# An expert layer's gate and up products in whole 512-column chunks, with SiLU, product and transposes at 512 columns, and the working area moved to a multiple of 64 bytes

## The chip, the cores and the metric

One Trainium2 chip, one of its cores. The metric is the device time of one execution of the whole program in microseconds (us), lower is better.

## The reference

One step of a two-layer language model on 256 prompt tokens and 8 decode tokens, 264 in all, model width 1024, all in fp32. Each layer has a mixer (differential attention beside a state-space model), a cross-attention to a memory of 256 rows, and a channel part, each followed by a residual and a layer norm. The channel part of layer 0 is a dense SwiGLU of width 2816. That of layer 1 is a mixture of 8 experts with the two best experts of each token, and it is this part that the change touches:

```
def _swiglu(x, w_gu, w_down):
    g, u = jnp.split(x @ w_gu, 2, axis=-1)
    return (jax.nn.silu(g) * u) @ w_down

def _moe(x, w_router, w_exp_gu, w_exp_down):
    ...
    for e in range(N_EXPERTS):
        out = out + _swiglu(x, w_exp_gu[e], w_exp_down[e]) * gate[..., e:e + 1].astype(x.dtype)
```

`w_exp_gu` is 8 x 1024 x 5632 (the first 2816 columns are gate, the others up), `w_exp_down` is 8 x 2816 x 1024: 34.6 MB of weights for each expert.

## The kernel before

The engines run programs written out by hand and meet on semaphores. The first 960 us or so are the two mixers, the cross-attentions and the dense SwiGLU; the eight experts follow, one after the other, each in the same loop body (`expert` on every engine).

**Weights in chunks.** SyncE (SP) streams an expert's weights into a ring of six slots of 2 MB: 11 gate/up chunks (positions p = 0 to 10) and 6 down chunks (p = 11 to 16, the last one half as large). Gate/up chunk i holds 256 gate columns and the 256 up columns that belong to them, for all 1024 rows, fetched by two DMAs (`load`, L800 to L805), so that each contiguous run in memory is 256 words, 1 KB. A slot is loaded again when PE has used its chunk up (`expert_chunk_used`).

**Two parts of each weight.** To get fp32 products from the faster fp32r format, each chunk is split in halves of 2048 words per partition. ScalarE (ACT) rounds a half into one of three buffers (`high_part`, L1772), VectorE (DVE) subtracts that from the original in place (`low_part`, L2155), and TensorE (PE) takes three matmuls for each 128 rows: high x high, low activations x high weights, high activations x low weights (`product`). The three `high` buffers tie the engines together: ACT may fill the buffer of half h only when PE has used half h-3 up.

**One expert on PE.** `gate_up(f)` multiplies the expert's up to 128 gathered tokens (the stationary operands `xg_high`, `xg_low`) with chunk f (the moving operand, 512 columns): 24 matmuls into one of two PSUM banks in turn, of which columns 0 to 255 are gate and 256 to 511 up. ACT takes SiLU of the gate half into `sg` (`silu`, L1783), DVE multiplies it with the up half into `hh` (`multiply`, L2170), PE turns the result with two 128-column transposes into a T bank (`transpose_h`, L1220, after the next chunk's matmuls), ACT and DVE take the high and the low part of that (`take_h`, L1787; `low_of_h`, L2178) for the down product. `sg`, `hh` and the T banks have two buffers each. Then `down(0..5)` makes the output rows from the down chunks. In the first four chunks PE also scatters the previous expert's rows to their tokens (`scatter_before`, with moving operand `SelT`), and DVE adds them (`add_scattered`, L2160). At the end of an expert, ACT and DVE scale and split the down result (`ye_high` L1808, `ye_low` L2206).

**The next expert's tokens.** DVE makes a selection matrix (`next_slots`, L2139) at p = 5, PE multiplies it with the token numbers beside the transposes of f = 6, DVE writes `slot_token` (L2176), and GpSimd (POOL) fetches the rows with an indirect DMA (L973). PE transposes them before `down(4)`.

**Order on ACT and DVE.** For each position p both run `high_part(p)` or `low_part(p)` first, then the small work: `silu(p-1)` or `multiply(p-1)`, then `take_h(p-2)` or `low_of_h(p-2)`.

**Memory.** `sb()` puts the tensors one after the other. `arena` is the working area that holds, among others, `xg_high`, `xg_low`, `sg`, `hh`, `he_high`, `he_low`, `ye_high` and `SelT` in this part, and `x_high`, `x_low`, `h_high`, `h_low` in the dense SwiGLU. It begins right behind the 4-byte `slot_token`, which takes 32 bytes of each partition; so it begins 32 bytes behind a multiple of 64. `ring`, `R`, `SQ` and `memT` (the `high` buffers) begin at multiples of 64.

Of the kernel before, what the change touches and what calls it, by code (L numbers as in the profile page):

```python
# [27 lines left out]
I32 = mybir.dt.int32  # L28
ALU = mybir.AluOpType
# [3 lines left out]
P = 128  # L33
# [26 lines left out]
SLOT = 4096  # L60
EPOS = NGU + NDN + 1
# [326 lines left out]
def build(nc, a, outs, lots=SLOTS, always=False):  # L388
# [3 lines left out]
    with ExitStack() as ctx:  # L392
# [51 lines left out]
        slot_token = sb("slot_token", [P, 1], I32)  # L444
        x_rows = nc.dram_tensor("x_rows", [T, D], F32).ap()
        arena = sb("arena", [P, ARENA])
        banks = [ctx.enter_context(nc.psum_tensor(f"bank{i}", [P, 512], F32)) for i in range(8)]
# [79 lines left out]
        sg = carve(2 * GU).rearrange("p (s n) -> p s n", s=2)  # L527
        hh = carve(2 * GU).rearrange("p (s n) -> p s n", s=2)
# [156 lines left out]
        def _(sp):  # L685
# [362 lines left out]
        TOKEN_STEP = 6  # L1048
        SUM_BANKS = GU_BANKS + T_BANKS

        def expert_products(pe, mm, tr, warm):
# [39 lines left out]
            def expert(e, c):  # L1091
# [28 lines left out]
                def scatter_matrix():  # L1120

                    pe.wait_ge(T_done, i * NGU + NGU - 1)
                    pe.wait_ge(T_low, i * NGU + NGU - 1)
                    for t in range(3):
                        tr(T_BANKS[1][0:lots, t * P:(t + 1) * P], Sel[:, t, 0:lots], P)
                    for t in range(3):
                        last = mm(T_BANKS[1][0:lots, 3 * P:3 * P + 1], GSel[:, t, 0:lots], one_col[:], t == 0, t == 2)
                    last.then_inc(scatter_full, 1)

                def transpose_h(f):  # L1130
                    pe.wait_ge(h_ready, i * NGU + (f + 1))
                    if f >= 2:
                        pe.wait_ge(T_done, i * NGU + (f - 1))
                        pe.wait_ge(T_low, i * NGU + (f - 1))
                    for s in range(2):
                        last = tr(T_BANKS[f % 2][:, s * lots:(s + 1) * lots],
                                  hh[0:lots, f % 2, s * P:(s + 1) * P], lots)
                    if f == TOKEN_STEP:
                        pe.wait_ge(next_sel_ready, i + 1)
                        for t in range(3):  # L1140
                            last = mm(T_BANKS[f % 2][0:lots, 3 * P:3 * P + 1], next_sel[:, t, 0:lots],
                                      const[:, C_TOK + t:C_TOK + t + 1], t == 0, t == 2)
                    last.then_inc(T_full, 1)

                def down(d):
                    p = NGU + d
                    f_last = min(4 * d + 3, FT - 1) // 2
                    pe.wait_ge(T_done, i * NGU + (f_last + 1))
                    pe.wait_ge(T_low, i * NGU + (f_last + 1))
# [13 lines left out]
                for f in range(NGU):  # L1163
# [588 lines left out]
        def expert_activations(act):  # L1752
# [22 lines left out]
            def expert(e, c):  # L1775
                i = expert_no(e, c)

                def silu(f):
                    act.wait_ge(gu_full, i * NGU + (f + 1))
                    if f >= 2:  # L1780
# [4 lines left out]
                def take_h(f):  # L1785
                    act.wait_ge(T_full, i * NGU + (f + 1))
                    S.activation(he_high[:, 2 * f:2 * f + 2, 0:lots],  # L1787
                                 T_BANKS[f % 2][:, 0:2 * lots].rearrange("p (s n) -> p s n", s=2),
                                 ACT.Copy).then_inc(T_done, 1)

                for p in range(1, NGU + NDN):
                    high_part(e, c, p)
                    if 1 <= p <= NGU:
                        silu(p - 1)
                    if 2 <= p <= NGU + 1:
                        take_h(p - 2)
                    if p == NGU + 3:
                        act.wait_ge(scatter_full, i + 1)
                        S.activation(slot_gate[0:lots], T_BANKS[1][0:lots, 3 * P:3 * P + 1], ACT.Copy).then_inc(gate_ready, 1)
                        S.activation(SelT[0:lots, :], T_BANKS[1][0:lots, 0:T], ACT.Copy).then_inc(scatter_ready, 1)  # L1800
# [323 lines left out]
        def expert_elementwise(dve):  # L2124
# [37 lines left out]
            def expert(e, c):  # L2162
                i = expert_no(e, c)

                def multiply(f):
                    dve.wait_ge(sg_ready, i * NGU + (f + 1))
                    if f >= 2:

                        dve.wait_ge(T_full, i * NGU + (f - 1))
                    V.tensor_tensor(hh[0:lots, f % 2, :], sg[0:lots, f % 2, :], GU_BANKS[f % 2][0:lots, GU:2 * GU],  # L2170
                                    ALU.mult).then_inc(h_ready, 1)

                def low_of_h(f):
                    dve.wait_ge(T_done, i * NGU + (f + 1))
                    if f == TOKEN_STEP:
                        V.tensor_copy(slot_token[0:lots], T_BANKS[f % 2][0:lots, 3 * P:3 * P + 1]  # L2176
                                      ).then_inc(token_ready, 1)
                    V.tensor_tensor(he_low[:, 2 * f:2 * f + 2, 0:lots],  # L2178
                                    T_BANKS[f % 2][:, 0:2 * lots].rearrange("p (s n) -> p s n", s=2),
                                    he_high[:, 2 * f:2 * f + 2, 0:lots], ALU.subtract).then_inc(T_low, 1)  # L2180

                for p in range(1, NGU + NDN):
                    low_part(e, c, p)
                    if 1 <= p <= NGU:
                        multiply(p - 1)
# [5 lines left out]
                    if 2 <= p <= NGU + 1:  # L2191
                        low_of_h(p - 2)
                    if p == TOKEN_STEP - 1:
# [596 lines left out]
```

## Time and profile before

| | us |
|---|---|
| three runs, median | 1812.07 |
| three runs, lowest and highest | 1811.1 and 1814.3 |
| the profiled execution, whole time | 1809.09 |
| the profiled execution, span from first to last instruction | 1807.2 |

The profile is of one execution. Its span is 1807.2 us, and 1.9 us of its time lie outside it. "Busy" is the time in which an engine had an instruction running; matmuls are pipelined, each is shown some 0.4 us long while the next one starts after 0.23 us, so for PE the distance from start to start is the cost. "Idle before" and "waited for" name what ended an engine's wait. The expert part runs from about 977 to 1784 us.

### The profile page before, as it was taken

What the parts mean: (1) busy time and instruction counts of PE and PEld (TensorE: products, weight loads), DVE (VectorE), ACT (ScalarE), POOL (GpSimd) and SP (SyncE); (2) the same over time, 40 slices, a digit from 0 to 9 for tenths busy, and PEclk for the clock granted to TensorE, in tenths of its full rate; (3) what the DMA queues carried; (4) which work ended last, traced back from release to release, by engine and by line L of the source; (5) the groups of instructions that cost most, each with busy time, mean ns of one, the idle gap of its engine ahead of it and who ended that gap; (6) DMA issues with size and microseconds to landing.
All of it is one profiled execution on the core that took longest, in us unless ns stands there. A gap on an engine that the chain in (4) does not pass through costs nothing.

```text
span 1807.2 us, 24014 instructions
## 1 busy us (share of the span) xinstructions
PE 1760.1 (97%) x8760; PEld 1360.8 (75%) x8760; DVE 1225.6 (68%) x1739; ACT 852.8 (47%) x978; POOL 112.2 (6%) x120
## 2 busy tenths in 40 slices
PE   7999999999999999999999999999999999999998
PEld 4646587789999565568677878878888878878786
DVE  2687636255544288543626989898988989898984
ACT  1122211154442122302205777777777777777774
POOL 0530000000000332000001000000000000000000
PEclk9999999999999999999998999999999999999999
DMA  9556544845526455563682989999999999999980
GB/s 323 183 199 212 215 185 169 285 158 181 175 83 228 137 185 171 187 262 123 233 279 96 358 279 356 345 348 352 349 376 324 377 324 363 337 350 352 348 335 26
DMA packets 300436, 459.34 MB, mean 254 GB/s; under 512 B 10879, under 2 KB 213817, under 8 KB 300343
## 3 DMA queue, kind: packets, MB, share of 16 engines
q1 hardware_dynamic: 294630, 442.63, 71.6%
q0 software_dynamic: 3424, 11.50, 1.9%
q10 hardware_dynamic: 2304, 4.20, 0.6%
q8 instruction: 47, 0.77, 0.2%
q14 instruction: 31, 0.25, 0.0%
HBM read 444.97 MB, written 13.46 MB: 254 GB/s over the span
## 4 chain that ended last, share of the span: by engine, by line
PE 86%; DVE 7%; ACT 3%; issue 1%; DMA 1%; SPq 1%; POOL 0%; ACTq 0%; DVEq 0%; POOLq 0%
PE bank L1216 83%; PE bank L1220 3%; DVE arena L2682 1%; DVE ring_low L2155 1%; ACT high L1772 1%; DMA out<-mem_rows 1%; DVE R L2296 1%; ACT L1772 0%; ACT arena L1840 0%; POOL arena L964 0%; ACT ye_high L1808 0%; ACT SQ L1861 0%; DVE st L2654 0%; DVE st L2575 0%; SPq L727 0%
## 5 line engine op out<-in xcount | busy, mean ns | idle before, releaser
L2155 DVE TENSOR_TENSOR ring_low<-ring,high 128x2048 fp32r<-128x2048 f32 x264 | 603.0, 2292 | 87.0 <-ACT high L1772 84.0
L1772 ACT ACTIVATE high<-ring 128x2048 fp32r<-128x2048 f32 x264 | 505.3, 1917 | 110.7 <-PE bank L1216 101.5
L1216 PE MATMUL bank<-high,xg_high 128*128 128x512 f32 x704 | 285.0, 405 | 6.2 <-DVE ring_low L2155 5.8
L1216 PE MATMUL bank<-ring_low,xg_high 128*128 128x512 f32 x704 | 278.5, 396 | 0.0
L1216 PE MATMUL bank<-high,xg_low 128*128 128x512 f32 x704 | 278.2, 395 | 0.0
L1216 PEld LDWEIGHTS bank<-high,xg_high 128*128 128x128 f32 x704 | 132.4, 188 | 36.3 <-DVE ring_low L2155 7.3
L1216 PEld LDWEIGHTS bank<-ring_low,xg_high 128*128 128x128 f32 x704 | 132.2, 188 | 31.7
L1216 PEld LDWEIGHTS bank<-high,xg_low 128*128 128x128 f32 x704 | 132.5, 188 | 28.4
L1840 ACT ACTIVATE arena<-bank 128x512 f32<-128x512 f32 (+3 forms) x95 | 46.4, 525 | 218.4 <-PE bank L1216 142.8
L1216 PE MATMUL bank<-high,he_high 128*128 128x512 f32 x352 | 141.8, 403 | 0.0
L1216 PE MATMUL bank<-ring_low,he_high 128*128 128x512 f32 x352 | 139.2, 396 | 0.0
L1216 PE MATMUL bank<-high,he_low 128*128 128x512 f32 x352 | 139.1, 395 | 0.0
L2273 DVE TENSOR_TENSOR ring_low<-ring,high 128x2048 fp32r<-128x2048 f32 (+1 forms) x32 | 71.1, 2225 | 92.6 <-ACT high L1849 92.6
L1216 PE MATMUL bank<-xT,ring 128*128 128x264 f32 x512 | 120.3, 391 | 0.8 <-ACT xT L1876 0.8
L1216 PE MATMUL bank<-SQ,ring 128*128 128x264 f32 x512 | 116.6, 391 | 0.9 <-issue 0.7
L1216 PE MATMUL bank<-ring,xT 128*128 128x512 f32 x256 | 116.5, 613 | 0.0
L1216 PE MATMUL bank<-ring,memT 128*128 128x512 f32 x256 | 113.3, 595 | 0.0
L1216 PEld LDWEIGHTS bank<-SQ,ring 128*128 128x128 f32 x512 | 98.1, 192 | 18.7 <-DVE SQ L2643 0.9
L1216 PEld LDWEIGHTS bank<-xT,ring 128*128 128x128 f32 x512 | 95.2, 190 | 21.9 <-issue 4.4
L1216 PE MATMUL bank<-x_high,ring_low 128*128 128x264 f32 x352 | 99.9, 284 | 0.0
L1849 ACT ACTIVATE high<-ring 128x2048 fp32r<-128x2048 f32 (+1 forms) x32 | 59.6, 1864 | 82.9 <-PE bank L1216 82.0
L1216 PEld LDWEIGHTS bank<-ring,xT 128*128 128x128 f32 x256 | 49.3, 196 | 62.6 <-issue 62.5
(327 smaller groups left out, 2613.2 us busy)
## 6 DMA issues: line engine op xcount, KB each, us to landing
ring<-in_w_exp_gu SPq DMA_DIRECT2D x176, 1024.0 KB, 11.3
ring<-in_w_exp_down SPq DMA_DIRECT2D x40, 2048.0 KB, 14.2
ring<-in_w_in SPq DMA_DIRECT2D x12, 2048.0 KB, 9.7
ring<-in_w_ffn_gu SPq DMA_DIRECT2D x22, 1024.0 KB, 8.5
ring<-in_w_ckv SPq DMA_DIRECT2D x8, 2048.0 KB, 8.6
ring<-in_cache_mem_k SPq DMA_DIRECT2D x16, 1024.0 KB, 8.1
ring<-in_cache_mem_v SPq DMA_DIRECT2D x16, 1024.0 KB, 6.6
ring<-in_cache_attn_k SPq DMA_DIRECT2D x32, 256.0 KB, 3.5
```

Of the source, the lines that this page charges most:

```text
L1216: return M.matmul(out, lhsT, rhs, start=start, stop=stop)
L1220: return M.transpose(out, in_, ident[0:n, 0:n])
L1772: S.activation(high_bufs[h % HIGH_BUFS][:], ring[:, s, j * HALF:(j + 1) * HALF], ACT.Copy).then_inc(split_high, 1)
L1840: emptied_after(name, S.activation(dst, src(bk), func))
L1849: S.activation(high, ring[:, s, part], ACT.Copy).then_inc(ffn_high, 1)
L2155: V.tensor_tensor(ring_low[:, s, part], ring[:, s, part], high_bufs[h % HIGH_BUFS][:], ALU.subtract).then_inc(split_low, 1)
L2273: V.tensor_tensor(ring_low[:, s, part], ring[:, s, part], high, ALU.subtract).then_inc(ffn_low, 1)
L2296: V.scalar_tensor_tensor(R[:, k, :], R[:, k, :], col_g(l, i, k), stat[:], ALU.mult, ALU.mult).then_inc(scaled.sem, 1)
L2682: ins = V.scalar_tensor_tensor(ctmp[:, (2 * t + j) * MD:(2 * t + j + 1) * MD], Kb[:, t, h * MD:(h + 1) * MD], 1.0, bk[:, j * MD:(j + 1) * ...
```

## The change

- Gate/up chunks 0 to 9 hold 512 columns of one kind: even ones gate, odd ones up, in pairs. Each is fetched by two DMAs of four 128-row blocks each, with contiguous runs of 512 words, 2 KB. Chunk 10 holds the last 256 gate and 256 up columns as before.
- An expert has PAIRS = 6 pairs q. The gate product of a pair is always in bank 0, the up product in bank 1 (for the last pair both in bank 0). SiLU, product, transposes (four 128-column ones in a row) and the two copies from the T bank work on 512 columns, 6 times instead of 11. `sg` and `hh` have one buffer.
- ACT takes `silu(q)` at odd p and `take_h(q)` at p = 2q+3 (12 for the last), DVE `multiply(q)` at even p and `low_of_h(q)` at p = 2q+3. PE transposes pair q after the gate chunk of pair q+1.
- Token numbers ride with the last pair's transposes (after `down(0)`) instead of f = 6, and `next_slots` is at p = 8 instead of 5. `scatter_matrix` uses T bank 0 instead of 1.
- `slot_token` is declared behind `arena`, which so begins at a multiple of 64 bytes. `ring`, `R`, `SQ`, `memT` stay where they were.

```diff
+PAIRS = (NGU + 1) // 2
...
-        slot_token = sb("slot_token", [P, 1], I32)
         x_rows = nc.dram_tensor("x_rows", [T, D], F32).ap()
         arena = sb("arena", [P, ARENA])
+        slot_token = sb("slot_token", [P, 1], I32)
...
-        sg = carve(2 * GU).rearrange("p (s n) -> p s n", s=2)
-        hh = carve(2 * GU).rearrange("p (s n) -> p s n", s=2)
+        sg = carve(2 * GU)
+        hh = carve(2 * GU)
...
+                    if i < NGU - 1:
+                        d = ring[:, s, :].rearrange("p (k n) -> p k n", k=KT)
+                        c0 = (i // 2) * 2 * GU
+                        for j in range(2):
+                            sp.dma_start(d[:, 4 * j:4 * j + 4, :], gu[:, 4 * j:4 * j + 4, i % 2, c0:c0 + 2 * GU]
+                                         ).then_inc(landed[s], 16)
+                        return
...
+        def tiles_of(q):
+            return min(4, FT - 4 * q)
+
+        def taken_at(q):
+            return min(2 * q + 3, NGU + 1)
...
-                        pe.wait_ge(h_ready, i * NGU + (f - 1))
+                        pe.wait_ge(h_ready if f % 2 else sg_ready, i * PAIRS + f // 2)
...
-                    for s in range(2):
-                        last = tr(T_BANKS[f % 2][:, s * lots:(s + 1) * lots],
-                                  hh[0:lots, f % 2, s * P:(s + 1) * P], lots)
-                    if f == TOKEN_STEP:
+                    for n in range(tiles_of(q)):
+                        last = tr(T_BANKS[q % 2][:, n * lots:(n + 1) * lots], hh[0:lots, n * P:(n + 1) * P], lots)
+                    if q == PAIRS - 1:
...
-                    if f:
-                        transpose_h(f - 1)
+                    if f and f % 2 == 0:
+                        transpose_h(f // 2 - 1)
                 down(0)
-                transpose_h(NGU - 1)
+                transpose_h(PAIRS - 1)
...
-                def silu(f):
-                    act.wait_ge(gu_full, i * NGU + (f + 1))
-                    if f >= 2:
-
-                        act.wait_ge(h_ready, i * NGU + (f - 1))
-                    S.activation(sg[0:lots, f % 2, :], GU_BANKS[f % 2][0:lots, 0:GU], ACT.Silu).then_inc(sg_ready, 1)
+                def silu(q):
+                    n = P * tiles_of(q)
+                    act.wait_ge(gu_full, i * NGU + (2 * q + 1))
+                    if q >= 1:
+
+                        act.wait_ge(h_ready, i * PAIRS + q)
+                    S.activation(sg[0:lots, 0:n], GU_BANKS[0][0:lots, 0:n], ACT.Silu).then_inc(sg_ready, 1)
...
-                    if 1 <= p <= NGU:
-                        silu(p - 1)
-                    if 2 <= p <= NGU + 1:
-                        take_h(p - 2)
+                    if p <= NGU and p % 2:
+                        silu(p // 2)
+                    for q in range(PAIRS):
+                        if p == taken_at(q):
+                            take_h(q)
...
-                    if 1 <= p <= NGU:
-                        multiply(p - 1)
+                    if 2 <= p <= NGU and (p % 2 == 0 or p == NGU):
+                        multiply((p - 1) // 2)
...
-                    if p == TOKEN_STEP - 1:
+                    if p == NGU - 3:
                         next_slots(bass.ds(e + 1, 1))
```

How the order moves, at two places. First ACT in the loop body of an expert, between chunk positions 5 and 6. Before, each position has two roundings (`high`), a SiLU (into `arena`) and a copy (`he_high`), 256 columns each:

```order
L1772 ACTIVATE high1_66<-ring 128x2048 [waits first_half_used]
L1779 REGISTER_ALU
L1783 ACTIVATE arena<-bank1 128x256 [waits h_ready,gu_full]
L1787 ACTIVATE he_high_59<-bank2 128x256 [waits T_full]
L1766 REGISTER_ALU
L1772 ACTIVATE high2_67<-ring 128x2048 [waits gu_full,landed0]
L1040 REGISTER_ALU
L1772 ACTIVATE high0_65<-ring 128x2048 [waits first_half_used]
L1779 REGISTER_ALU
L1783 ACTIVATE arena<-bank0 128x256 [waits h_ready,gu_full]
L1787 ACTIVATE he_high_59<-bank3 128x256 [waits T_full]
```

In the changed kernel, at positions 3 to 5, there are four roundings in a row between two such pairs, and the pairs are 512 columns wide:

```order
L1796 ACTIVATE arena<-bank0 128x512 [waits h_ready]
L1801 ACTIVATE he_high_59<-bank2 128x512 [waits T_full]
L1784 ACTIVATE high2_67<-ring 128x2048 [waits gu_full,landed3]
L1048 REGISTER_ALU
L1784 ACTIVATE high0_65<-ring 128x2048 [waits first_half_used]
L1778 ISA
L1050 REGISTER_ALU [waits landed4]
L1784 ACTIVATE high1_66<-ring 128x2048 [waits gu_full]
L1048 REGISTER_ALU
L1784 ACTIVATE high2_67<-ring 128x2048 [waits first_half_used]
```

The SiLU and the copy of the even positions are gone; those of the odd ones have grown, and stand together ahead of the same rounding.

Second PE, where chunk 4 of an expert ends (`high`, `ring_low`: weights; `xg_high`, `xg_low`: tokens). Before, two transposes (`const,arena`) stand between any two chunks:

```order
L1216 MATMUL bank0<-high0_65,xg_low_58 128x512
L1216 MATMUL bank0<-ring_low_68,xg_high_57 128x512
L1131 REGISTER_ALU
L1220 MATMUL bank3<-const,arena 128x128 [waits T_low,T_done,h_ready]
L1220 MATMUL bank3<-const,arena 128x128
L1096 REGISTER_ALU [waits h_ready]
L1216 MATMUL bank1<-high1_66,xg_high_57 128x512 [waits split_low]
```

Now four stand there:

```order
L1228 MATMUL bank0<-ring_low_68,xg_high_57 128x512
L1232 MATMUL bank3<-const,arena 128x128 [waits h_ready]
L1232 MATMUL bank3<-const,arena 128x128 x3
L1110 REGISTER_ALU [waits h_ready]
L1228 MATMUL bank1<-high1_66,xg_high_57 128x512 [waits split_low]
```

Behind chunk 5 stands none: the next gate chunk follows with a wait for SiLU alone. The number of matmuls and of transposes is the same.

## Rows read from the trace of the kernel before

**Rows 1.** The page, part 1: busy us, share of the span, instructions.

```profile
PE 1760.1 (97%) x8760; PEld 1360.8 (75%) x8760; DVE 1225.6 (68%) x1739; ACT 852.8 (47%) x978; POOL 112.2 (6%) x120
```

**Rows 2.** Windows view, the stretch of one expert, with granted clock and DMA.

```profile
core 0: us, PE busy (x) PEld busy (x) DVE busy (x) ACT busy (x) POOL busy (x), PEclk, DMA share, GB/s
1083.50:1183.90 100.40, 99.52 (x457) 80.92 (x457) 89.66 (x79) 74.86 (x64) 1.03 (x1) 1.00 1.03 350
```

**Rows 3.** Waits, 1200 to 1400 us: us in total, times, longest us.

```profile
ACT high L1772 <- PE bank L1216: 25.3, 36, 1.9
DVE ring_low L2155 <- ACT high L1772: 20.7, 46, 1.8
...
PE bank L1216 <- DVE ring_low L2155: 1.7, 2, 0.8
```

**Rows 4.** Timelines of ACT and DVE where an expert begins: start us, us, engine, line.

```profile
1277.42 1.27 ACT L1808 ACTIVATE ye_high<-bank,arena 128x512 fp32r<-128x512 f32 x2 [0.88 <-PE bank L1216]
1278.71 1.28 ACT L1772 ACT_TABLE_LOAD   x1
1280.00 3.72 ACT L1772 ACTIVATE high<-ring 128x2048 fp32r<-128x2048 f32 x2
...
1281.95 4.50 DVE L2155 TENSOR_TENSOR ring_low<-ring,high 128x2048 fp32r<-128x2048 f32 x2 [1.76 <-ACT high L1772]
```

**Rows 5.** Timeline of PE over one gate/up chunk, from its second matmul on.

```profile
1209.02 0.40 PE L1216 MATMUL bank<-high,xg_low 128*128 128x512 f32 x1
...
1213.69 0.40 PE L1216 MATMUL bank<-high,xg_high 128*128 128x512 f32 x1
...
1214.39 0.38 PE L1220 MATMUL bank<-const,arena 128*128 128x128 f32 x2
...
1214.84 0.39 PE L1216 MATMUL bank<-high,xg_low 128*128 128x512 f32 x1
```

**Rows 6.** Timelines of ACT and DVE beside that chunk.

```profile
1208.76 0.39 ACT L1783 ACTIVATE arena<-bank 128x256 f32<-128x256 f32 x1 [0.88 <-PE bank L1216]
1209.04 0.38 ACT L1787 ACTIVATE he_high<-bank 128x256 fp32r<-128x256 f32 x1
1209.31 1.92 ACT L1772 ACTIVATE high<-ring 128x2048 fp32r<-128x2048 f32 x1
...
1211.37 2.29 DVE L2155 TENSOR_TENSOR ring_low<-ring,high 128x2048 fp32r<-128x2048 f32 x1
```

**Rows 7.** Groups by shape: copies and subtractions from a bank at 512 columns.

```profile
L1840 ACT ACTIVATE arena<-bank 128x512 f32<-128x512 f32 x58 | 32.1, 596 | 155.9 <-PE bank L1216 86.2 <-PE bank L1220 68.4 <-ACT mem_rows L1840 1.2
...
L1759 ACT ACTIVATE xg_high<-bank 128x512 fp32r<-128x512 f32 x18 | 9.7, 588 | 6.2 <-PE bank L1216 6.2
...
L2147 DVE TENSOR_TENSOR xg_low<-bank,xg_high 128x512 fp32r<-128x512 f32 x18 | 11.6, 684 | 1.8 <-ACT xg_high L1759 1.8
```

**Rows 8.** DMA view, 1200 to 1300 us in 40 slices.

```profile
GB/s 348 347 349 349 348 348 349 347 348 370 411 411 406 413 411 405 413 406 413 410 406 162 18 334 350 238 367 357 342 353 332 355 352 348 348 349 350 348 348 348
```

**Rows 9.** The next expert's rows: the gather's time, and DVE and PE timelines.

```profile
DMA to landing us min/median/max: 7.0/7.6/7.8
...
1251.49 0.42 DVE L2178 TENSOR_TENSOR he_low<-bank,he_high 128x256 fp32r<-128x256 f32 x1
...
1267.94 1.04 PE L1220 MATMUL bank<-const,xT 128*128 128x128 f32 x8
```

**Rows 10.** Other PE timelines (dense SwiGLU; an fp32 product), and weight loads by shape.

```profile
405.06 0.28 PE L1216 MATMUL bank<-x_high,ring_low 128*128 128x264 f32 x1
...
405.42 0.28 PE L1216 MATMUL bank<-x_high,ring_low 128*128 128x264 f32 x1
...
117.13 7.13 PE L1216 MATMUL bank<-ring,xT 128*128 128x512 f32 x16
...
L1216 PEld LDWEIGHTS bank<-high,xg_low 128*128 128x128 f32 x704 | 132.5, 188 | 28.4
...
L1216 PEld LDWEIGHTS bank<-x_high,ring_low 128*128 128x128 f32 x352 | 66.1, 188 | 0.0
```

More of the change, by code:

```diff
@@ L1047, in build @@
         GU_BANKS, T_BANKS, Y_BANKS, X_BANKS = banks[0:2], banks[2:4], banks[4:6], banks[6:8]
-        TOKEN_STEP = 6
+        def tiles_of(q):
+            return min(4, FT - 4 * q)
+        def taken_at(q):
+            return min(2 * q + 3, NGU + 1)
         SUM_BANKS = GU_BANKS + T_BANKS
@@ L1146, in down @@
                     p = NGU + d
-                    f_last = min(4 * d + 3, FT - 1) // 2
-                    pe.wait_ge(T_done, i * NGU + (f_last + 1))
-                    pe.wait_ge(T_low, i * NGU + (f_last + 1))
+                    pe.wait_ge(T_done, i * PAIRS + (d + 1))
+                    pe.wait_ge(T_low, i * PAIRS + (d + 1))
                     for j, h in halves_of(p):
@@ L1776, in expert, with take_h @@
                 i = expert_no(e, c)
-                def silu(f):
-                    act.wait_ge(gu_full, i * NGU + (f + 1))
-                    if f >= 2:
-                        act.wait_ge(h_ready, i * NGU + (f - 1))
-                    S.activation(sg[0:lots, f % 2, :], GU_BANKS[f % 2][0:lots, 0:GU], ACT.Silu).then_inc(sg_ready, 1)
[L1785 to L1788, printed above, removed]
+                def silu(q):
[4 more added lines that the diff above has]
+                    S.activation(sg[0:lots, 0:n], GU_BANKS[0][0:lots, 0:n], ACT.Silu).then_inc(sg_ready, 1)
+                def take_h(q):
+                    n = tiles_of(q)
+                    act.wait_ge(T_full, i * PAIRS + (q + 1))
+                    S.activation(he_high[:, 4 * q:4 * q + n, 0:lots],
+                                 T_BANKS[q % 2][:, 0:n * lots].rearrange("p (s n) -> p s n", s=n),
                                  ACT.Copy).then_inc(T_done, 1)
@@ L1792, in expert @@
                     high_part(e, c, p)
-                    if 1 <= p <= NGU:
-                        silu(p - 1)
-                    if 2 <= p <= NGU + 1:
-                        take_h(p - 2)
+                    if p <= NGU and p % 2:
[3 more added lines that the diff above has]
+                            take_h(q)
                     if p == NGU + 3:
                         act.wait_ge(scatter_full, i + 1)
-                        S.activation(slot_gate[0:lots], T_BANKS[1][0:lots, 3 * P:3 * P + 1], ACT.Copy).then_inc(gate_ready, 1)
-                        S.activation(SelT[0:lots, :], T_BANKS[1][0:lots, 0:T], ACT.Copy).then_inc(scatter_ready, 1)
+                        S.activation(slot_gate[0:lots], T_BANKS[0][0:lots, 3 * P:3 * P + 1], ACT.Copy).then_inc(gate_ready, 1)
+                        S.activation(SelT[0:lots, :], T_BANKS[0][0:lots, 0:T], ACT.Copy).then_inc(scatter_ready, 1)
                 take_gathered(x_groups_before(e, c) + KT)
@@ L2163, in expert, with multiply, low_of_h @@
                 i = expert_no(e, c)
[L2165 to L2176, printed above, removed]
+                def multiply(q):
+                    n = P * tiles_of(q)
+                    up = GU_BANKS[1][0:lots, 0:n] if q < PAIRS - 1 else GU_BANKS[0][0:lots, GU:2 * GU]
+                    dve.wait_ge(gu_full, i * NGU + min(2 * q + 2, NGU))
+                    dve.wait_ge(sg_ready, i * PAIRS + (q + 1))
+                    if q >= 1:
+                        dve.wait_ge(T_full, i * PAIRS + q)
+                    V.tensor_tensor(hh[0:lots, 0:n], sg[0:lots, 0:n], up, ALU.mult).then_inc(h_ready, 1)
+                def low_of_h(q):
+                    n = tiles_of(q)
+                    dve.wait_ge(T_done, i * PAIRS + (q + 1))
+                    if q == PAIRS - 1:
+                        V.tensor_copy(slot_token[0:lots], T_BANKS[q % 2][0:lots, 3 * P:3 * P + 1]
                                       ).then_inc(token_ready, 1)
-                    V.tensor_tensor(he_low[:, 2 * f:2 * f + 2, 0:lots],
-                                    T_BANKS[f % 2][:, 0:2 * lots].rearrange("p (s n) -> p s n", s=2),
-                                    he_high[:, 2 * f:2 * f + 2, 0:lots], ALU.subtract).then_inc(T_low, 1)
+                    V.tensor_tensor(he_low[:, 4 * q:4 * q + n, 0:lots],
+                                    T_BANKS[q % 2][:, 0:n * lots].rearrange("p (s n) -> p s n", s=n),
+                                    he_high[:, 4 * q:4 * q + n, 0:lots], ALU.subtract).then_inc(T_low, 1)
                 for p in range(1, NGU + NDN):
                     low_part(e, c, p)
-                    if 1 <= p <= NGU:
-                        multiply(p - 1)
+                    if 2 <= p <= NGU and (p % 2 == 0 or p == NGU):
+                        multiply((p - 1) // 2)
                     if p == 1:
@@ L2190, in expert @@
                             add_scattered(e, c, k, X_BANKS[k % 2])
-                    if 2 <= p <= NGU + 1:
-                        low_of_h(p - 2)
-                    if p == TOKEN_STEP - 1:
+                    for q in range(PAIRS):
+                        if p == taken_at(q):
+                            low_of_h(q)
+                    if p == NGU - 3:
                         next_slots(bass.ds(e + 1, 1))
```

19 lines of the change are left out of this document (10 added, 9 removed).

## The prediction, written before the changed kernel ran

> **What bounds the kernel now.** I read the page first: PE is busy for 1760.1 of 1807.2 us, far ahead of DVE and ACT [rows 1]. The change touches the expert part alone, apart from the place of the working area, so the windows view of one expert comes next: 100.4 us, of which PE is busy 99.5, DVE 89.7, ACT 74.9, at full granted clock (1.00, the 2.4 GHz level), while the DMA engines show 1.03 of their time and 350 GB/s [rows 2]. Three resources look full, and the busy shares do not say which one sets the pace. The waits do [rows 3]: in two experts ACT waits 36 times for PE (a `high` buffer that is still in use), DVE waits 46 times for ACT, and PE waits for DVE twice, 0.8 us each. So everything is paced by PE, and PE stops once in an expert. Nobody there is shown waiting for a load.
>
> The one stop is the start of an expert [rows 4]: ACT can scale the last down result only when PE has made it (1277.42), then loads an activation table (1278.71, 1.28 us), then rounds chunk 1 (1280.00), DVE subtracts (1281.95, 2.25 us for the first half), and PE, which has chunk 0 and four scatter matmuls to do meanwhile, runs out 0.8 us before that ends.
>
> Between stops PE's time is a count of matmuls. In [rows 5] matmul 2 of a chunk starts at 1209.02 and matmul 22 at 1213.69: 4.67 / 20 = 0.2335 us from start to start. Matmul 2 of the next chunk starts at 1214.84, 5.82 us after. 24 matmuls take 5.60 of that, and two transposes the remaining 0.22, 0.11 each.
>
> **The sum, against the profiled execution (1809.09 us, 3.0 under the median of three, 1812.07).** I work out the difference and add it to the median.
>
> *Matmuls and transposes.* An expert has 33 halves of 12 matmuls, 396, before and after, and 22 transposes. The only thing that could differ is the cost of going over from matmuls to transposes and back, 11 times before and 6 times now. But the 5.82 us leave nothing for it: 24 x 0.2335 + 2 x 0.11 is all of it [rows 5]. Since these readings are good to 0.01 us or so in a chunk, 5 fewer changes in each of 8 experts are worth 0, between -1.2 and +1.2 us (0.03 each way, 40 times). **0.**
>
> *ACT, at odd positions.* SiLU and copy of 512 columns stand together ahead of a rounding that PE waits for in the end. Before [rows 6], behind the end of a chunk come SiLU 0.39, copy 0.38 and from 1209.31 the rounding, 1.92; DVE subtracts from 1211.37 to 1213.66; PE needs the half for matmul 1 of its next chunk, some 0.3 us ahead of matmul 2 at 1214.84 [rows 5], at 1214.53: 0.87 us in hand. At 512 columns copies from a bank take 0.60 and 0.59 [rows 7], so the rounding starts 0.42 later. PE now has four transposes there instead of two and needs the half 0.22 later. What is in hand falls to 0.87 - 0.42 + 0.22 = 0.67 us. No stop, so **0**; covered by PE's own chunk. The even positions have neither SiLU nor copy, there the rounding starts 0.77 earlier than before.
>
> *DVE.* A 512-column product or subtraction takes 0.68 [rows 7] against 2 x 0.42 for 256 [rows 9]. Odd positions have one (`low_of_h`), even ones one (`multiply`) and, at p = 8, three selections. DVE saves 5 x 0.16 us in an expert, and what it saves it waits for ACT: **0**. PE's new waits have long slack. For an odd chunk from the third on it waits for `multiply` of the pair before, which DVE does within some 2.5 us of the even chunk's 5.6 us; for an even chunk it waits for a SiLU that is a whole chunk old. With one `sg` and one `hh`, SiLU of pair q waits for the product of q-1, a chunk earlier, and the product for transposes that are a chunk old. Behind each of these waits stands the next rounding or subtraction, so if one were late, PE would be late with it; none is by over 2 us of slack.
>
> *The tail of the expert.* The last transposes carry the six small matmuls for the token numbers; they move, they don't multiply. The table load, the scaling and the rounding of [rows 4] are where they were, in the same order: the stop of 0.8 us stays, **0**. The token numbers come later: DVE writes them where it did the last `low_of_h`, at about 1251.5 + 0.7, PE wants the gathered rows at 1267.94, and the gather takes 7.0 to 7.8 us from its issue [rows 9]. Even with 1 us between, it lands near 1261, 7 us early. **0.** Nothing is moved past another transfer on SP; POOL has only the gather.
>
> *Loads.* Runs of 2 KB instead of 1 KB. In the gate/up stage the queue moves 348 GB/s, in the down stage, with 4 KB runs, 410, and once in an expert it falls to 162 and 18 because the loads have caught up and wait for a slot [rows 8]. The loads thus end each expert ahead of PE. Faster loads only make that hole wider. If they should be slower, the hole (some 1.6 of 40 slices of 2.5 us, 4 us in an expert) is what they may lose first. **0.**
>
> *The working area's place.* The stationary `xg` and `he` tiles and the moving `SelT` lie in it; the moving weights don't. Nothing in the trace shows the same matmul at both places, so I bound it. The most: matmuls get as fast as fp32 ones go for the same columns, 16 rows in 7.13 us, 0.446 each, half of it 0.223 for a pass of 512 columns [rows 10]; (0.2335 - 0.223) x 3168 = 33 us less. The other end I set as far away, 33 us more, for want of a row that excludes it. I take 0, by the two rows that are nearest: weight loads of `xg_low`, in the working area, take 188 ns, and so do those of `ring_low`, which is at a multiple of 64 already [rows 10]; and the dense SwiGLU's matmuls, with stationary operands at multiples of 64, need 0.36 / 3 = 0.120 us for 264 columns, or 0.455 ns a column, as much as the experts' 0.2335 for 512, 0.456. **0.**
>
> The Trainium skill (TensorE: Matmul & The Clock Gate, section "Back-to-back issue gap") gives start to start as the columns over 2.4 GHz plus 2.5 ns, 216 ns for 512. This trace doesn't agree: it shows 0.2335. By the page's figure there would be 17.5 ns in each matmul for something that slows them here, and if the alignment were that, the sum would be some 55 us less, an estimate.
>
> Sum: 0, so **1812.1 us**.
>
> **The rivals.** (A) *The working area's place does matter.* For it: the matmuls stand above the fp32 rows, and 3168 of them sit on the path, so that 1 ns each is 3.2 us. Against it: the two rows of 188 and the equal cost of a column. That equality is good to about 1%, 2 ns, which is 6 us: **1806**. If the whole bound came, 1779. By the page's 216 ns the time would come out there or lower; this trace's equal cost of a column speaks against it.
>
> (B) *ACT's wide pairs overrun (slower).* Place: the first half of each chunk behind an odd position, five in an expert. It decides when SiLU, copy and hand-overs take over 0.67 us more than I reckon, say because the copy must wait for the fourth transpose and for its own semaphore, or SiLU at 512 is dearer than a plain copy. An overrun by 0.3 us is 0.3 x 5 x 8 = 12 us: **1824**. For it: DVE and ACT have 0.87 us in hand today, not more. Against it: the sum above leaves 0.67 of it.
>
> (C) *Loads or the gather come late (slower).* 2 KB runs of two DMAs that now each span four row blocks could be dearer. To be felt they must eat the hole and the ring's lead, some 5 us in an expert; each us beyond costs 8: 1 us gives **1820**. Against it: rows with longer runs go at 410.
>
> (D) *The expert's start gets shorter.* If DVE or ACT came to the end of an expert earlier, up to 7 x 0.8 = 6 us would go, **1806.5**. Against it: the chain starts at PE's last matmul, which the change doesn't move.
>
> **Chances.** A measurement of this kernel can tell about 0.2%, 3.6 us, from no change. Forecast 0.69; A 0.15; B 0.07; C 0.05; D 0.04. Faster: A and D, 0.19; within 0.2%: 0.69; slower: 0.12. The range takes the forecast's own 1808.5 to 1815.7, reaches down over A's and D's 1806 and leaves out A's far part (0.06) and B and C (0.12): **1804.5 to 1816**.
>
> **What would show it.** Right: the expert's stretch is again 100.3 to 100.4 us; start to start 0.2335; four transposes cost 0.43; PE waits once in an expert, 0.8 us, for DVE; ACT's rounding behind an odd position starts near 0.4 us later but DVE still ends over 0.5 us before PE needs it; the DMA row above 348 GB/s in the gate/up stage with a wider hole. Wrong: a start to start under 0.232 (A), a second PE wait for `ring_low` in each pair (B), ACT waiting for a landing or PE for `xT` (C), or the 0.8 us gone (D).

## The result: faster by 0.8%, and the profile after

| | before | changed kernel |
|---|---|---|
| median of four runs | 1811.92 us | 1798.59 us |
| lowest and highest | 1811.1 and 1814.3 | 1792.82 and 1799.22 |
| ratio of the times | | 0.9916, 95% interval 0.9896 to 0.9935 |
| the profiled execution, span | 1807.2 | 1790.7 |
| the same kernel timed again (run a2_changed) | 1812.6 (11 runs) | 1797.28 (6 runs), ratio 0.9919, 0.9900 to 0.9938 |

The profiled execution of the changed kernel is the fastest of its four, at a mean clock of 0.993 where the others show 0.988 and 0.989; below, spans are compared with spans and medians with medians. The prediction was 1812.1, with a range that ended at 1804.5. It was wrong.

The page, part 1, of the changed kernel, and its windows view over one expert, from the end of PE's stop to the end of the next:

```profile
PE 1743.2 (97%) x8760; PEld 1362.3 (76%) x8760; DVE 1214.5 (68%) x1659; ACT 845.4 (47%) x898; POOL 111.8 (6%) x120
```

```profile
core 0: us, PE busy (x) PEld busy (x) DVE busy (x) ACT busy (x) POOL busy (x), PEclk, DMA share, GB/s
1082.31:1180.54 98.23, 97.24 (x457) 80.95 (x457) 88.23 (x68) 73.89 (x54) 1.03 (x1) 1.00 0.97 358
```

Against [rows 2] the expert is 2.1 us shorter (98.23 for 100.3 to 100.4) with as many instructions on PE (457) at the same granted clock (1.00). PE's busy time fell by 2.3 us. Eight experts make 17 us, and the spans of the two profiled executions differ by 16.5: the whole gain is there. The medians differ by less, 13.3 us and, timed again, 15.3. In the pair timed again the changed kernel's executions were granted a mean clock of 0.9905 and those of the kernel before 0.9916; 0.0011 of 1800 us is 2 us, an estimate, and would cover the difference. Why they were granted less is not shown. What DVE and ACT saved (1.4 and 1.0 us) is theirs alone, since PE still paces both, as the waits from 1200 to 1400 us show:

```profile
ACT high L1784 <- PE bank L1228: 36.6, 48, 1.8
DVE ring_low L2170 <- ACT high L1784: 19.7, 31, 1.7
...
PE bank L1228 <- DVE ring_low L2170: 2.0, 2, 1.0
```

As in [rows 3], PE waits twice in two experts, for DVE. It waits longer, 1.0 us instead of 0.8. So the gain isn't a wait that went; it lies between the stops. The timeline of PE over a gate chunk, behind which four transposes stand:

```profile
1210.73 0.39 PE L1228 MATMUL bank<-ring_low,xg_high 128*128 128x512 f32 x1
...
1214.81 0.39 PE L1228 MATMUL bank<-ring_low,xg_high 128*128 128x512 f32 x1
...
1215.49 0.39 PE L1228 MATMUL bank<-ring_low,xg_high 128*128 128x512 f32 x1
1215.72 0.60 PE L1232 MATMUL bank<-const,arena 128*128 128x128 f32 x4
...
1217.78 0.39 PE L1228 MATMUL bank<-high,xg_low 128*128 128x512 f32 x1
```

18 matmuls take 4.08 us, **0.2267 each, where [rows 5] showed 0.2335**. Same instruction, same shape, same clock, other pace. Behind the transposes it is not there at once: from 1215.49 to 1217.78 are 8 matmuls and 4 transposes, 2.29 us; 8 x 0.2267 and 4 x 0.11 leave 0.04 us over.

The stop at an expert's start, by the timelines of ACT, DVE and PE:

```profile
1271.89 1.27 ACT L1823 ACTIVATE ye_high<-bank,arena 128x512 fp32r<-128x512 f32 x2 [0.80 <-PE bank L1228]
1273.18 1.28 ACT L1784 ACT_TABLE_LOAD   x1
1274.47 3.72 ACT L1784 ACTIVATE high<-ring 128x2048 fp32r<-128x2048 f32 x2
...
1276.42 4.49 DVE L2170 TENSOR_TENSOR ring_low<-ring,high 128x2048 fp32r<-128x2048 f32 x2 [1.69 <-ACT high L1784]
...
1278.77 0.49 PE L1228 MATMUL bank<-high,xg_high 128*128 128x512 f32 x1 [1.00 <-DVE ring_low L2170]
```

From ACT's scaling to DVE's subtraction are 4.53 us, as in [rows 4]. The chain is what it was. PE, which has 24 matmuls to do beside it, is through with them 24 x 0.0066 = 0.16 us sooner, and waits that much longer.

The loads in the same 100 us as [rows 8], and the weight loads of `xg_low`:

```profile
GB/s 383 391 383 390 357 349 372 416 400 415 410 406 415 405 411 415 401 360 0 120 113 326 402 206 401 377 395 378 254 399 399 383 390 383 390 384 389 384 389 386
```

```profile
L1228 PEld LDWEIGHTS bank<-high,xg_low 128*128 128x128 f32 x704 | 132.3, 188 | 25.7
```

Gate/up loads move at 383 to 391 GB/s where they had 348, and the hole is wider (0, 120, 113). A weight load still shows 188 ns.

### The profile page after: what moved, and what is told of

Read it like the earlier page. It is cut to its first block, busy times and chain, and to the rows that moved or that the text cites. A ratio compares the mean times of both kernels' runs of the same rounds, so it can differ in the third digit from the quotient of the medians.

```text
span 1790.7 us, 23663 instructions
## 1 busy us (share of the span) xinstructions
PE 1743.2 (97%) x8760; PEld 1362.3 (76%) x8760; DVE 1214.5 (68%) x1659; ACT 845.4 (47%) x898; POOL 111.8 (6%) x120
## 4 chain that ended last, share of the span: by engine, by line
PE 85%; DVE 7%; ACT 4%; issue 1%; DMA 1%; SPq 1%; POOL 0%; ACTq 0%; DVEq 0%; POOLq 0%
PE bank L1228 83%; PE bank L1232 3%; DVE arena L2701 1%; DVE ring_low L2170 1%; ACT high L1784 1%; DMA out<-mem_rows 1%; DVE R L2315 1%; ACT L1784 1%; ACT arena L1855 0%; POOL arena L972 0%; ACT ye_high L1823 0%; ACT SQ L1876 0%; DVE st L2673 0%; DVE st L2594 0%; SPq L734 0%
## 5 line engine op out<-in xcount | busy, mean ns | idle before, releaser
L1228 PE MATMUL bank<-high,xg_high 128*128 128x512 f32 x704 | 278.1, 395 | 7.3 <-DVE ring_low L2170 7.0
L1228 PE MATMUL bank<-ring_low,xg_high 128*128 128x512 f32 x704 | 274.6, 390 | 0.0
L1228 PE MATMUL bank<-high,xg_low 128*128 128x512 f32 x704 | 274.2, 389 | 0.0
```

The source lines that it names most:

```text
L1228: return M.matmul(out, lhsT, rhs, start=start, stop=stop)
```

## The experiments

Places are told within 256 bytes. The moving weights, in `ring` and in the tensors that hold the `high` buffers, begin 128 bytes past a multiple of 256. The distance of a stationary tile is its place less theirs: before, the whole working area stood at 32; in the changed kernel it stands at 0. "18" is the time of 18 matmuls ahead of a group of transposes or other work, from starts in the timeline near 1200 to 1255 us (4.11 where the series is still coming back from the group before it); `xg` is gate and up, `he` is down. Every row is from one profiled execution. An expert's time is from stop to stop.

| run | distance of xg, of he | 18 with xg, with he, us | an expert, us | span, us |
|---|---|---|---|---|
| before | 32, 32 | 4.20 from [rows 5] | 100.35 | 1807.2 |
| changed | 0, 0 | 4.08, 4.11 | 98.23 | 1790.7 |
| e1_place | 0, 0 | 4.09, 4.08 | 98.46 | 1795.0 |
| e2_chunks | 32, 32 | 4.19, 4.19 | 100.31 | 1812.1 |
| e3_he_off | 0, 32 | 4.08, 4.20 | 98.99 | 1798.4 |
| e4_at_64 | 64, 64 | 4.20, 4.20 | 100.40 | 1811.7 |
| e6_at_512 | 128, 128 | 4.20, 4.19 | 100.16 | 1807.3 |
| e7_moving_off | 0 and 224 in turn | 4.13, 4.14 | 99.36 | 1803.5 |
| e8_all_by_128 | 0, 0 | 4.07, 4.11 | 98.19 | 1789.6 |
| e9_off_96_160 | 96, 160 | 4.22, 4.20 | 100.58 | 1813.2 |
| e10_off_192_224 | 192, 224 | 4.12, 4.20 | 99.42 | 1800.6 |
| e12_xg_low_off | high 0 and low 32, 0 | 4.20, 4.09 | 99.57 | 1803.5 |

Spans also differ by up to some 5 us in what lies ahead of the first stop of the experts, so the third and fourth columns decide.

### Which part of the change

**e1_place**: the kernel before, with this alone:

```
-        slot_token = sb("slot_token", [P, 1], I32)
         x_rows = nc.dram_tensor("x_rows", [T, D], F32).ap()
         arena = sb("arena", [P, ARENA])
+        slot_token = sb("slot_token", [P, 1], I32)
```

> The kernel before with one line moved: slot_token behind arena, so that arena begins at a multiple of 64 bytes; chunks, SiLU and transposes as before. Theory P (place): TensorE's 512-column matmuls go at 0.227 us from start to start instead of 0.2335, because their stationary operands lie in arena; 3168 of them give about 17 to 19 us, so some 1794 to 1797 us against 1812 in the same call, and one expert's stretch falls from 100.3 to about 98.2 us. Theory C (chunks): the spacing comes from the new chunks (half as many loads' runs, half as many small instructions beside the matmuls), so this kernel stays at 0.2335 us and 1812 us.

**e2_chunks**: the changed kernel, with these lines put back.

> The changed kernel with slot_token back ahead of arena, which so begins 32 bytes behind a multiple of 64; all of the chunk change stays. Theory P: 0.2335 us from start to start, the expert's stretch 100.3 us, no difference to the kernel before (1808.5 to 1815). Theory C: 0.227 us and 1799 us as in the changed kernel.

Timed in five rounds beside the kernel before (1812.94, 15 runs): e1_place 1800.06 (5 runs), ratio 0.9936, 0.9922 to 0.9949; e2_chunks 1812.02 (11 runs), 0.9998, 0.9989 to 1.0007. The windows of one expert of e1_place, then of e2_chunks:

```profile
1084.11:1182.57 98.46, 97.47 (x457) 80.80 (x458) 89.54 (x78) 74.80 (x64) 1.03 (x1) 1.00 1.04 356
```

```profile
1088.66:1188.97 100.31, 99.48 (x457) 81.00 (x457) 88.37 (x68) 73.91 (x54) 1.03 (x1) 1.00 0.95 350
```

The place of the working area gives nearly all, the chunks by themselves nothing. What is left to the chunks once the place is right is 98.46 - 98.23 = 0.23 us an expert, 1.8 us in eight: five groups of transposes fewer, at the 0.04 us each that showed above. The place alone is worth (100.35 - 98.46) x 8 = 15.1 us by the stretches and 12.9 by the medians. With the old place a group cost nothing over its transposes, and so e2_chunks gains nothing.

### Which operand, and is it 64 bytes

**e3_he_off**: the changed kernel with `carve(8)` (32 bytes) ahead of `he_high` and again behind `he_low`.

> The changed kernel with he_high and he_low alone moved by 32 bytes (8 unused words ahead of them and 8 behind), everything else in arena stays at multiples of 64. Theory P with stationary operands as the cause: the down matmuls (stationary he_high, he_low) go back to 0.2335 us, the gate and up matmuls (stationary xg_high, xg_low) stay at 0.227 us; 132 x 8 matmuls x 6 ns are 6.3 us more, about 1799 us in the profiled run where the changed kernel had 1792.8. A theory that some other tile in arena does it, or writes into it: both stay at 0.227 us.

PE's timeline of e3_he_off, over a stretch with `xg` and over one with `he`:

```profile
1203.04 0.39 PE L1230 MATMUL bank<-ring_low,xg_high 128*128 128x512 f32 x1
...
1207.12 0.39 PE L1230 MATMUL bank<-ring_low,xg_high 128*128 128x512 f32 x1
...
1249.53 0.40 PE L1230 MATMUL bank<-ring_low,he_high 128*128 128x512 f32 x1
...
1253.73 0.40 PE L1230 MATMUL bank<-ring_low,he_high 128*128 128x512 f32 x1
```

4.08 us against 4.20 in one run: the down matmuls, whose stationary tiles alone have moved, lose the quick pace, and the gate and up ones keep it.

**e4_at_64**: 64 bytes of padding ahead of `arena`. **e6_at_512**: 128 bytes (`slot_token` and a pad), which puts it at a multiple of 512.

> The changed kernel with 16 unused words ahead of arena, which so begins at an odd multiple of 64 bytes, not of 128. If 64 bytes are the unit that counts: 0.227 us for all, 1793 us in the profiled run. If 128 bytes are: between 0.230 and 0.2335 us, 1800 to 1809 us.

> The changed kernel with arena at a multiple of 512 bytes (it is 384 bytes behind one now). If 128 bytes are the whole unit: 0.227 us from start to start as now, stretch 98.2 us. If the steps went on (64 did nothing, 128 gave 6 ns): a spacing nearer to 0.216 us, up to 35 us less.

Their windows, e4_at_64 first:

```profile
1087.92:1188.32 100.40, 99.57 (x458) 81.02 (x458) 88.38 (x68) 73.93 (x54) 1.03 (x1) 1.00 0.95 350
```

```profile
1084.35:1184.51 100.16, 99.30 (x458) 81.14 (x458) 88.34 (x68) 73.91 (x54) 1.03 (x1) 1.00 0.95 351
```

A multiple of 64, and even of 512, is as slow as before (1813.65 and 1809.37 in one run each). The diff's "at a multiple of 64 bytes" describes the new place and isn't what makes it good.

**e7_moving_off**: the stationary tiles stay, two of the three moving `high` buffers start 32 bytes later.

> The changed kernel with two of the three high buffers moved by 32 bytes: the moving operand of two matmuls in three, in two halves out of three, is off a multiple of 128, the stationary ones stay. If the moving operand's place counts too: spacings in those halves go to 0.2335 us where high is moving, on average some 3 us an expert more (24 us). If only the stationary one's counts: 0.227 us in all halves of the experts; the dense SwiGLU, where high is the stationary operand, gets slower where it can.

99.36 us an expert, half way, so the moving operand's place counts too. The expectation's 3 us an expert was missed: it is 1.1, and all 372 matmuls at the slow pace would have made 2.5. In the halves that use the moved buffers, where two pairs in three are out of place, the mean spacing is 0.2314, not 0.2333; in those of the third buffer it comes down to 0.2267 after some 8 matmuls.

### Relative or absolute

Theory R: the two operands must begin at the same place within 256 bytes. Theory A: the stationary one must be 128 past a multiple of 256. Everything so far fits both.

**e8_all_by_128**: `slot_token` and a pad, 128 bytes in all, ahead of `ring`, the first of these tensors, so that everything moves together.

> Changed kernel with 128 bytes put ahead of the first working tensor and slot_token taken from behind the arena, so that the weight ring, the tiles of high halves and the arena all stand 128 bytes higher than in the changed kernel; their distances from each other stay. Theory R (matmuls are quick where the stationary and the moving operand begin at the same place within 256 bytes): everything stays as in the changed kernel, 227.3 ns from matmul to matmul with xg and he, 98.2 us an expert, 1793 us in the profile. Theory A (quick where the operands stand 128 bytes past a multiple of 256): 233.3 ns, 100.3 us, 1810 us.

Its windows view, one expert:

```profile
1081.53:1179.72 98.19, 97.20 (x457) 80.94 (x458) 88.25 (x68) 73.84 (x54) 1.03 (x1) 1.00 0.94 358
```

98.19 us: theory A falls. **e9_off_96_160** and **e10_off_192_224** (`carve(24)` or `carve(48)` ahead of `xg_high`, `carve(16)` or `carve(8)` ahead of `he_high`) fill in the distances:

> Changed kernel with xg_high and xg_low (the stationary tiles of gate and up) 96 bytes on and he_high and he_low (those of down) 160 bytes on from where they stand. Theory R in its plain form (only equality within 256 bytes is quick): 233.3 ns for both, 100.3 us an expert, 1810 us. If the distance itself grades the spacing, the two differ from 233.3: between 227.3 and 233.3, or above it. If a period of 64 or 32 bytes were enough after all, one of them is at 227.3.

> Changed kernel with xg_high and xg_low 192 bytes on and he_high and he_low 224 bytes on (32 bytes short of the same place within 256). Theory R in its plain form: 233.3 ns for both, 100.3 us an expert, 1810 us. If the cost grades with the distance, 224 bytes on would read as 32 bytes back and lie nearer to 227.3 than 192 does.

PE's timeline of e10_off_192_224:

```profile
1202.28 0.39 PE L1231 MATMUL bank<-ring_low,xg_high 128*128 128x512 f32 x1
...
1206.40 0.40 PE L1231 MATMUL bank<-ring_low,xg_high 128*128 128x512 f32 x1
...
1249.05 0.39 PE L1231 MATMUL bank<-ring_low,he_high 128*128 128x512 f32 x1
...
1253.25 0.39 PE L1231 MATMUL bank<-ring_low,he_high 128*128 128x512 f32 x1
```

So theory R in its plain form falls too. Distance 0 is the best, but 192 has two thirds of its gain (4.12 us, 0.229 each), while its neighbours 160 and 224 have the slow 4.20 and 96 is slowest (4.22). It isn't nearness either.

### The dense SwiGLU, and one operand in three

There the weights are the stationary operand, at distance 0 already, and the moving rows `x_high` and `x_low`, 264 words apart, shift by 32 bytes from row to row. (The expectation of e11 calls these rows stationary, with 256 moving columns; they are the moving operand, 264 columns wide. The pairs are the same.)

**e5_x_rows**: their rows 288 words apart, so that they alternate between distance 0 and 128.

> The changed kernel, and in layer 0's dense SwiGLU the two tiles of moving operands x_high and x_low get rows of 288 words instead of 264, so that every 128-row block begins at a multiple of 128 bytes (h_rows moves to another tile to make room). If the moving operand's place counts as the stationary one's does: 1056 matmuls of 264 columns go from 0.1215 to about 0.117 us, 4 to 5 us less, 1793 to 1795 us, and the h matmuls beside them stay at 0.122. If only the stationary operand's place counts (here weights, at multiples of 128 in both): 0.1215 us as before and no difference to the changed kernel.

**e11_x_high_320**: the rows of `x_high` all in place, those of `x_low` not (`x_low` and `h_rows` are moved to make room).

```
-        x_high = parts_in("x_high", "arena", 2 * FT * T, [KT, T])
+        x_high = parts_in("x_high", "arena", 2 * FT * T + 32, [KT, 320])
```

> Changed kernel in which the rows of x_high, the stationary tiles of the dense SwiGLU, are 320 words apart instead of the width of a row of tokens and begin at the place within 256 bytes at which the moving tiles begin; x_low stays at mixed places. Theory R: the 704 matmuls of the dense SwiGLU with x_high and 256 moving columns go from 121.5 to some 117.5 ns, about 2.8 us less in all, a median near 1795.5 us; those with x_low stay at 121.5. Theory A: the same, since that place is also 128 past a multiple of 256. If the dense SwiGLU is bound by something else, the stretch stays and the median is that of the changed kernel, 1798.

e5_x_rows 1796.65 (6 runs), beside 1797.28 for the changed kernel in the same call, which was

> The changed kernel once more, as the measure for the runs beside it: 1797 to 1800 us, expert's stretch 98.2 us.

e11_x_high_320 had 1795.58 (4 runs), ratio 0.9906, 0.9889 to 0.9922, within the changed kernel's own interval. In both, the dense matmuls kept their pace (mean 0.1217 and 0.1215 us, 0.1214 in the changed kernel). In e5 every other product was in place, in e11 two matmuls of every three, and nothing was gained: either the dense part is bound by something else, or a pair out of place spoils the series. Two runs tell these apart.

**e12_xg_low_off**: in the experts, `xg_low` alone 32 bytes on.

> Changed kernel with xg_low alone 32 bytes on (what lies behind it in the arena stands 256 bytes further, so at the same place within 256 as before). One of the three matmuls of a product in gate and up has then a stationary operand at another place than the moving one; the other two keep theirs. Theory O (each matmul pays for its own pair): mean spacing in gate and up 227.3 + 6 / 3 = 229.3 ns, with two of three intervals at 227; period some 98.9 us. Theory S (the quick pace is one of the whole series, and one pair in three that does not match breaks it): all three kinds at 231 to 234 ns, period some 99.5 us or more. In both, down stays at 227.4.

PE's timeline of e12_xg_low_off:

```profile
1206.52 0.40 PE L1228 MATMUL bank<-high,xg_high 128*128 128x512 f32 x1
1206.76 0.39 PE L1228 MATMUL bank<-high,xg_low 128*128 128x512 f32 x1
1206.99 0.40 PE L1228 MATMUL bank<-ring_low,xg_high 128*128 128x512 f32 x1
1207.22 0.40 PE L1228 MATMUL bank<-high,xg_high 128*128 128x512 f32 x1
```

0.240, 0.228 and 0.232 us by the trace's own nanoseconds, over and over: 0.700 for three, 0.2333 each, all that the whole working area out of place costs. A pair out of place is paid by the matmuls around it too.

**e13_dense_high_only**: e11 with `x_high` also in the place of `x_low`. The low half of the dense SwiGLU's input is left out of gate and up.

> The kernel of e11 in which the dense SwiGLU's gate and up take x_high also in the place of x_low, so that their middle term is wrong and the low half of the input is left out of it; the count and shapes of the matmuls are the same, and all three moving operands of a product now begin where the weights do, within 256 bytes. Theory S: 1056 matmuls go from 121.5 to some 117.5 ns, 4.2 us less before the experts begin. Theory O: two thirds of that should have shown in e11, where nothing did, so it expects nothing here: 121.5 ns.

PE's timelines in the dense SwiGLU, of e11_x_high_320 and of e13_dense_high_only:

```profile
404.86 0.29 PE L1228 MATMUL bank<-x_high,high 128*128 128x264 f32 x1
...
405.95 0.29 PE L1228 MATMUL bank<-x_high,high 128*128 128x264 f32 x1
```

```profile
404.78 0.40 PE L1228 MATMUL bank<-x_high,high 128*128 128x264 f32 x2
...
406.22 0.28 PE L1228 MATMUL bank<-x_high,high 128*128 128x264 f32 x1
```

9 matmuls in 1.09 us, 0.121 each; 12 in 1.44, 0.120 each, and in the trace's nanoseconds exactly 120 for 967 of 991, against a mean of 121.5. Theory S (the series) holds in its direction; its size here was 4 ns and is 1.5. One rival stands: e13 also gives two matmuls in a row the same two operands, and no run tells that from the place; for the dense part the cause is thus argued, and e12 alone shows the series. I had taken the 4 ns from `SelT` with `ye_high`, 117.5; but those alternate with `ye_low` at some 123, and the pair's mean is some 120. Reading one kind out of an alternating series was the mistake. A full alignment of the dense part would be worth 1056 x 1.5 ns = 1.6 us, less than a measurement of this kernel tells, so no such version was built. None of the runs is measurably faster than the changed kernel.

## Why the prediction was wrong

**The step that failed is *The working area's place*, taken at 0.** By itself it measured -15.1 us in the stretches of eight experts (e1_place; -12.9 by that run's medians), and with the chunks, which then gain too, -17.0. By the experiments' numbers, for the whole change: of an expert's 396 matmuls, 24 lie beside the chain of the stop, which didn't change; 372 x 6.6 ns = 2.46 us less; six groups of transposes give back 6 x 0.04 = 0.24; 2.2 us remain, and 2.12 were measured (100.35 to 98.23). The range that this step had worked out, 33 us either way, held it; the choice of 0 within it did not, and the final range cut that bound off at 1804.5. Both rows that I chose by were the wrong witnesses:

- *Weight loads at 188 ns in both places* [rows 10]. They still take 188 in the changed kernel, where the matmuls are 6.6 ns faster. The duration shown for a weight load doesn't hold the cost, which only the distance from start to start of the matmuls shows.
- *The dense SwiGLU costs as much a column, 0.455 against 0.456.* That was no control: its own operands are out of place (stationary weights in place, moving rows at places that shift by 32 bytes), and e13 shows that with all in place it still needs 0.120 for 264 columns, 0.4545 each, while the experts come to 0.2267 for 512, 0.443. The row was also read short: 0.120 is from one product of three matmuls, and the mean of the dense series before is 0.1214, 0.460 a column. Two slow series that agree say nothing of whether a faster one exists.

The bound was misread as well. The 7.13 us of the fp32 row [rows 10] reach to the end of its last matmul, which is shown 0.59 us long. By starts, matmul 2 and matmul 15 of that row, each the first of the two on its line, are 5.58 us apart, 0.4292 each:

```profile
117.66 1.02 PE L1216 MATMUL bank<-ring,xT 128*128 128x512 f32 x2
...
123.24 1.02 PE L1216 MATMUL bank<-ring,xT 128*128 128x512 f32 x2
```

Half of that is 0.2146, not 0.223, and the bound becomes (0.2335 - 0.2146) x 3168 = 60 us. (That half an fp32 matmul is a fair measure for an fp32r one is an assumption that no run tests.) The row held a second hint: its stationary tiles, in rows of `xT` 264 words apart, stand at eight different places, and its spacing stays at 0.429 throughout. So these fp32 matmuls don't pay for the place.

Rival A had the cause in part, that the place costs time on every matmul, and a third of the size: 1806 from 2 ns, since it, too, leaned on the second row. It took the place for an alignment, which e4_at_64 and e6_at_512 refute. Its own sign ("a start to start under 0.232") is what the profile shows.

**Matmuls and transposes**: 0 within 1.2 us either way was right for the kernel as it was read (e2_chunks: 0.9998) and became 1.8 us less once the place changed, just over that bound. A cost of going over, hidden in one state, was taken as a constant.

**ACT, at odd positions**: no stop, as forecast. Behind such a pair DVE begins, and PE's next chunk starts, at

```profile
1207.56 4.50 DVE L2170 TENSOR_TENSOR ring_low<-ring,high 128x2048 fp32r<-128x2048 f32 x2 [0.88 <-ACT high L1784]
...
1210.27 0.39 PE L1228 MATMUL bank<-high,xg_high 128*128 128x512 f32 x1
```

the first subtraction takes 2.29 us and ends at 1209.85, 0.42 us in hand. Forecast were 0.67; the faster chunk takes 24 x 0.0066 = 0.16 of that, so the reckoning was good to 0.1. Rival B falls.

**DVE** and **Loads**: 0, as forecast: DVE's saving went into its waits (1.4 us an expert, not the 5 x 0.16 of the reckoning, which counted one of a pair's two saved operations), faster loads into the hole; rival C falls. **The tail**: the chain stayed, but the stop grew from 0.83 to 1.00 us since PE got ahead of it, 0.16 us an expert that the faster matmuls don't bring; rival D falls.

The Trainium skill (TensorE: Matmul & The Clock Gate, section "Back-to-back issue gap") gives the 216 ns for 512 columns as the gap of a matmul by itself. Half of the fp32 row's spacing, 214.6, is close to it; the fp32r matmuls need 226.7 at their best in any run, so of the 17.5 ns in question 6.7 were the place and 10.7 stay unexplained.

## What to carry to other kernels

- Runs of 2 KB instead of 1 KB raised the gate/up loads from 348 to some 387 GB/s, and their landing came in 9.9 us in the median, where it was 11.3; this kernel has no use for it.
